# Output projection of a decoder layer on one NeuronCore: whole fp32 products, another order of token tiles, and earlier loads for the first two experts

## What is computed

```python
z = x @ w_in + b_in                       # q, k, v, conv pair, two gates
attn, conv = ...                          # dilated attention; depthwise conv
branch_c = silu(layer_norm(conv)) @ w_conv_out + b_conv_out
branch_a = attn @ w_attn_out
y = (g_a * branch_a + g_c * branch_c) @ w_o
h = layer_norm(DN_ALPHA * x + y)
# router: top 1 of 4 groups, then top 2 of its 8 experts, from fp32 logits
out = layer_norm(DN_ALPHA * h + moe(h))   # 32 SwiGLU experts, 1024 -> 512 -> 1024
```

## Time and profile before

| | us |
|---|---|
| median of 3 runs | 1113.03 (1111.85 to 1113.34) |
| profiled execution | 1111.08 |
| its span | 1109.3 |
| PE busy | 1021.5 (92%) |
| DVE busy | 624.5 (56%) |
| ACT busy | 286.8 (26%) |
| POOL busy | 217.2 (20%) |
| DMA queues, share of 16 engines | 69.3% |

### The profile page before, as it was taken

One profiled execution on the slowest core, in us unless ns is written; L12 is line 12 of the kernel. 1 busy time (PEld: TensorE's weight loads), 2 busy tenths in 40 slices (PEclk: granted clock), 3 DMA queues, 4 the chain that ended last, 5 costly groups with the idle time before them and its releaser, 6 DMA issues. The chain is left out here.

```text
span 1109.3 us, 30843 instructions
## 1 busy us (share of the span) xinstructions
PE 1021.5 (92%) x12960; PEld 792.5 (71%) x12960; DVE 624.5 (56%) x1386; ACT 286.8 (26%) x600; POOL 217.2 (20%) x193
## 2 busy tenths in 40 slices
PE   9999999999999899995999999999899998989880
PEld 8999998899997678874566665656565655656650
DVE  2699999810126728477367655445445453535435
ACT  3322321232225662011122222122121212212123
POOL 2453440232210014002111112111111212110100
PEclk9999999999998999996899999999999999999995
DMA  8467834136423521326999999999999999999624
GB/s 293 166 252 269 313 116 162 67 138 219 151 86 139 204 82 64 127 81 245 390 372 409 402 418 403 403 403 380 395 358 401 380 357 378 345 376 348 259 74 164
DMA packets 45696, 293.55 MB, mean 265 GB/s; under 512 B 11519, under 2 KB 15231, under 8 KB 26173
## 3 DMA queue, kind: packets, MB, share of 16 engines
q1 hardware_dynamic: 22285, 163.96, 38.3%
q10 hardware_dynamic: 12624, 102.63, 22.8%
q0 software_dynamic: 10720, 25.98, 7.9%
HBM read 286.83 MB, written 41.12 MB: 296 GB/s over the span
## 5 line engine op out<-in xcount | busy, mean ns | idle before, releaser
L978 PE MATMUL ps<-region_b,scratch 128*32 128x256 f32 x2976 | 174.7, 389 | 24.3 <-DMA region_b<-in_gate_up_rows 24.3
L978 PE MATMUL ps<-region_a,scratch 128*32 128x256 f32 x3168 | 180.3, 381 | 10.5 <-DMA region_a<-in_gate_up_rows 10.5
L995 PE MATMUL ps<-z_conv_gates,x_columns 128*32 128x256 f32 x3072 | 172.1, 379 | 0.0
L1718 DVE STREAM_TRANSPOSE scratch<-x_columns 32x256 f32<-32x256 f32 x384 | 165.8, 432 | 9.7 <-DMA x_columns<-h_rows,token_rows 3.6
L978 PEld LDWEIGHTS ps<-region_b,scratch 128*32 128x32 f32 x2976 | 107.5, 112 | 85.5 <-issue 26.3
L978 PEld LDWEIGHTS ps<-region_a,scratch 128*32 128x32 f32 x3168 | 113.8, 111 | 71.0 <-issue 15.8
L995 PEld LDWEIGHTS ps<-z_conv_gates,x_columns 128*32 128x32 f32 x3072 | 110.4, 110 | 55.3
L1375 DVE SCALAR_TENSOR_TENSOR z_conv_gates<-scratch,column_vectors,z_conv_gates 128x512 f32<-128x512 f32 x240 | 143.0, 673 | 0.0
L1724 DVE SCALAR_TENSOR_TENSOR x_columns<-ps,column_vectors,x_columns 128x128 f32<-128x128 f32 x96 | 33.7, 351 | 166.8 <-ACT x_columns L1272 165.0
L1272 ACT ACTIVATE x_columns<-ps 128x128 f32<-128x128 f32 x96 | 26.6, 277 | 377.6 <-PE ps L978 377.6
L579 PE MATMUL ps<-z_split,region_b_split 128*128 128x272 f32 x384 | 111.2, 290 | 0.0
(11 more groups left out here) (266 smaller groups left out, 1337.9 us busy)
## 6 DMA issues: line engine op xcount, KB each, us to landing
region_b<-in_gate_up_rows SPq DMA_DIRECT2D x21, 2048.0 KB
region_a<-in_gate_up_rows ACTq DMA_DIRECT2D x21, 2048.0 KB, 42.2
z_conv_gates<-in_down_rows SPq DMA_DIRECT2D x32, 1024.0 KB
z_conv_gates<-in_down_rows ACTq DMA_DIRECT2D x32, 1024.0 KB
region_a<-in_gate_up_rows SPq DMA_DIRECT2D x12, 2048.0 KB
region_b<-in_w_in_pairs SPq DMA_DIRECT2D x20, 1024.0 KB, 5.0
region_b<-in_gate_up_rows ACTq DMA_DIRECT2D x10, 2048.0 KB
region_b<-in_cache_tiles POOLq DMA_DIRECT2D x16, 768.0 KB, 4.9
```

Of the source, the lines that this page charges most:

```text
L978: last = pe.matmul(ps[j * R:(j + 1) * R, r, 0:2 * QF], ecols[s][:, r, 4 * c + k, :], w[:, k, j, :], start=c + k == 0, stop=c + k == 4)
L995: last = pe.matmul(ps[j * R:(j + 1) * R, RB + r, 0:QD], hcols[:, r, k * R:(k + 1) * R], w[:, k, j, :], start=k == 0, stop=k == KF - 1)
L1718: last = ve.transpose(ecols[s][q * R:(q + 1) * R, r, :, :].rearrange("p k c -> p (k c)"), xg[s][r * R:(r + 1) * R, q * QD:(q + 1) * QD])
```

## The change

- w_o is made in one fp32 product for each k (no high and low parts, no ACT casts and DVE subtractions). The sum of the two branches goes to `gc[m]`.
- The small tile is second: the tiles are now 128 (tile 0), 32 (tile 1), 128, 128, 128 rows. Its product is made in four column quarters of 256, one for each group of 32 PSUM partitions (`small_out`).
- Tiles 0 and 2 are made together, k by k, after all eight `br_used`. The norm of the last tile is no longer cut in two parts.
- Both gate-and-up halves of expert 1 are issued beside the second one of expert 0, after `merged` 6, and the down halves of experts 0 and 1 after `merged` 8. Gate and up and down of expert 2 still wait for `gathered[0]`.

The core of the diff:

```diff
-TILES = [(t * P, min(P, N - t * P)) for t in range((N + P - 1) // P)]
+SMALL = 1
+TILES = [(r * P, P) for r in range(SEQ // P)]
+TILES.insert(SMALL, (SEQ, NS))
...
                 if t == 1:

-                    sp_e.wait_ge(x_split, XQ + 6)
+                    sp_e.wait_ge(merged, 6)
                     load_gates(0, 0, 1)
-            sp_e.wait_ge(y_ps, NTT + 1)
-            for s in range(2):
-                sp_e.wait_ge(krow_stored[s], 16 * 3)
-            load_gates(1, 1, 0)
+                    load_gates(1, 1, 0)
+                    sp_e.wait_ge(merged, KD)
+                    for s in range(2):
+                        sp_e.wait_ge(krow_stored[s], 16 * 3)
+                    load_down(0, 0)
+                    load_down(1, 1)
+            sp_e.wait_ge(y_ps, NTT)

             sp_e.wait_ge(gathered[0], 16)
-            load_down(0, 0)
             load_gates(2, 2, 0)
-            load_down(1, 1)
             load_down(2, 2)
...
                     for k in ks:
-                        pe.matmul(out, ga_hi[k][:, c0:c0 + n], wo_hi[:, k, cols], start=k == 0, stop=False)
-                        pe.matmul(out, ga_hi[k][:, c0:c0 + n], wo_lo[:, k, cols], start=False, stop=False)
-                        last = pe.matmul(out, ga_lo[k][:, c0:c0 + n], wo_hi[:, k, cols], start=False, stop=k == KD - 1)
+                        last = pe.matmul(out, gc[k][:, c0:c0 + n], wo[:, k, cols], start=k == 0, stop=k == KD - 1)
+            def small_out():
+                c0, n = TILES[SMALL]
+                for k in range(KD):
+                    for j in range(GROUPS):
+                        last = pe.matmul(ps[j * R:(j + 1) * R, 6, 0:QD], gc[k][:, c0:c0 + n], wo[:, k, j * QD:(j + 1) * QD],
+                                         start=k == 0, stop=k == KD - 1)
+                return last
...
-            pe.wait_ge(br_used, KD - 1)
+            pe.wait_ge(br_used, KD)
+            pe.wait_ge(wo_loaded, 16)
             for k in range(KD - 2):
...
+                pe.wait_ge(merged, k + 1)
+                for t in (0, 2):
                     rows_out(t, [k])
+            pe.wait_ge(merged, KD)
+            rows_out(0, range(KD - 2, KD)).then_inc(y_ps, 1)
+            small_out().then_inc(y_ps, 1)
+            rows_out(2, range(KD - 2, KD)).then_inc(y_ps, 1)
+
+            turn_tile(0)
             pe.wait_ge(y_used, 1)
+            rows_out(3, range(KD), [0])
             logit_tile(0)
             turn_tile(1)
+            rows_out(3, range(KD), [1]).then_inc(y_ps, 1)
             logit_tile(1)
             turn_tile(2)
+            pe.wait_ge(y_used, 3)
+            rows_out(4, range(KD), [0])
             logit_tile(2)
             turn_tile(3)
+            rows_out(4, range(4), [1])
             logit_tile(3)
+            rows_out(4, range(4, KD), [1]).then_inc(y_ps, 1)
...
             norm_tile(0)
             norm_tile(1)
             norm_tile(2)
             route_tile(0)
+            norm_tile(3)
             route_tile(1)
-            norm_tile(3)
             route_tile(2)
+            route_tile(3)
             norm_tile(4)
             rank_tiles(0, NTT - 1, 1)
             route_tile(4)
...
-                po.tensor_tensor(ga[m], ga[m], gc[m], ALU.add).then_inc(merged, 1)
+                po.tensor_tensor(gc[m], ga[m], gc[m], ALU.add).then_inc(merged, 1)
```

More of the change, by code:

```diff
@@ L285, in build @@
         spare_row = route(NE)
-        COUNT_BANK = [3] * (NTT - 1) + [7]
-        LAST_ORDER = [NTT - 1, *range(NTT - 1)]
+        COUNT_BANK = [0] * (NTT - 1) + [6]
+        OUT_BANK = {0: 0, 2: 2, 3: 0, 4: 2}
+        LAST_ORDER = [SMALL, *(t for t in range(NTT) if t != SMALL)]
         unused_rows = z2[:, 0:D]
@@ L875, in logit_tile @@
                 for k in range(KD):
-                    last = pe.matmul(ps[0:n, 6 + t % 2, 0:36], hcol[:, k, 0:n], wrv[:, k, :], start=k == 0, stop=k == KD - 1)
+                    last = pe.matmul(ps[0:n, 7 - t % 2, 0:36], hcol[:, k, 0:n], wrv[:, k, :], start=k == 0, stop=k == KD - 1)
                 last.then_inc(lg_ps, 1)
@@ L883, in counts @@
                 for u in range(t):
-                    pe.matmul(out, onesb, mb[:, u, :], start=u == 0, stop=False)
+                    m = TILES[u][1]
+                    pe.matmul(out, onesb[0:m, :], mb[0:m, u, :], start=u == 0, stop=False)
                 return pe.matmul(out, beforeb[0:n, :], mb[0:n, t, :], start=t == 0, stop=True)
@@ L889, in listed @@
                 for k in range(2):
-                    last = pe.matmul(ps[0:BLK, 2, 0:NE], ohr_f[0:n, k * NTT + t, :], ohn[0:n, k, t, :],
+                    last = pe.matmul(ps[0:BLK, 1, 0:NE], ohr_f[0:n, k * NTT + t, :], ohn[0:n, k, t, :],
                                      start=t == 0 and k == 0, stop=t == NTT - 1 and k == 1)
@@ L951, in _ @@
             for t, (c0, n) in enumerate(TILES):
-                last = pe.matmul(ps[:, 3, NTT * NE:(NTT + 1) * NE], onesb[0:n, :], mb[0:n, t, :], start=t == 0, stop=t == NTT - 1)
+                last = pe.matmul(ps[:, 0, NTT * NE:(NTT + 1) * NE], onesb[0:n, :], mb[0:n, t, :], start=t == 0, stop=t == NTT - 1)
             last.then_inc(cnt_ps, 1)
@@ L1236, in _ @@
             columns_out(0)
+            root(2)
             columns_out(1)
-            for t in range(2, NTT):
-                root(t)
-                columns_out(t)
-            ac.wait_ge(y_ps, NTT + 1)
-            for s in range(2):
-                ac.wait_ge(krow_stored[s], 16 * 3)
-            def load_gates(e, s):
-                ac.dma_start(gu_place[s][1], gu_d[bass.ds(2 * e + 1, 1)].rearrange("o p x -> p (o x)")).then_inc(gu_loaded[s][1], 16)
-            def load_down(e, s):
-                ac.dma_start(dn_place[s][:, 2048:4096], dn_d[bass.ds(e, 1), 1].rearrange("o p x -> p (o x)")).then_inc(dn_loaded[s], 16)
-            load_gates(1, 1)
+            root(3)
+            columns_out(2)
+            columns_out(3)
+            root(4)
+            columns_out(4)
+            ac.wait_ge(y_ps, NTT)
             ac.wait_ge(rmax, 1)
```

113 lines of the change are left out of this document (36 added, 77 removed).

## The result

The changed kernel takes **1145.0 us** (median of 4 runs, 1137.7 to 1146.3), the one before, on the same chip, 1112.7 us: ratio 1.0273, 95% interval 1.0234 to 1.0312. By the ratio it is 30 us slower. The prediction, 1114.8 in a range of 1109.5 to 1119.5, missed. Executions far outside the rest (one of e1 with 1352.5 us, one of the kernel before with 3684.6 us) are left out of all comparisons.

What follows compares the result with a forecast made beforehand. PE was taken to eat a stock of weights, then go at the pace of HBM, with the DMA queues as the bound. A chain 8.2 us later less 6.4 us of stock put 1.8 on 1113.03: 1114.8 us, range 1109.5 to 1119.5.

Steps and rivals of the forecast that it cites:

- the base of the sum: Whole kernel before the change: median 1113.03 us, to which the forecast added its net.
- 8.2 - 6.4 us: Routing chain 8.2 us late, less 6.4 us taken for a stock of weights larger by 4.0 us.
- the first part: What bounds the kernel: PE takes 15.54 us per expert from 545 us, later 17.78 at the pace of HBM.
- the last rival: Early loads don't come early, or their traffic slows PE's instruction fetch: 8.2 us lost whole, 1121.2; chance 0.03.
- w_o stage: PE's w_o products: start 437.15, sum 67.0 us, end 504.1, no new stall inside.
- Chain and clock: After w_o, at half clock: turn 2.0, logits 3.6, row lists at 523.8, 8.2 us late.
- With the lead-in unchanged: Row lists to expert 3's load: stays 29.4 us, so that load is asked for at 553.2 instead of 545.0.
- Early loads: 10 MiB from about 428 us, done by 455; 4 MiB leave the later stream, stock larger by 4.0 us, worth 6.4.
- The hole in the traffic: DMA queues before expert 3's load: idle from about 547 to 553.2, some 6 us.
- First wait for weights at expert 12 to 14: Expert loop: sign of a right forecast, PE's first wait for weights at expert 12 to 14 instead of 10.
- The net, 1.8 us: Whole kernel: 8.2 us of later chain less 6.4 us of stock, 1.8 us later.
- the forecast's two nearest cases, 1114.8 and 1117.2: Whole kernel: forecast itself, 1114.8, chance 0.42; slower rival, stock worth only its 4.0 us, 1117.2, chance 0.33.

Runs made afterwards that it cites:

- e1: The change with 99 semaphore increments on PE in two gaps of the routing chain, loop body back at place 138; 1124.6 us.
- e13: The change with 49 products of 16 columns and one increment behind keep_running, loop body at place 138; 1117.3 us, ratio 1.0052 to the kernel before.
- e2: The kernel before with 157 semaphore increments on PE in three gaps, loop body at place 39 as in the change; 1145.7 us.
- e7: e8 with both early moves taken back: expert 1's gates after the last `y_ps`, downs of 0 and 1 after the gather; 1121.1 us.
- e8: The change with the loops of PE and SP over experts 3 to 26 written out; 1113.5 us.
- e6: The kernel before with the loops of PE and SP over experts 3 to 26 written out; 1111.2 us.
- e9: e8 with PE kept busy by products in the gaps of the routing chain; 1110.0 us.
- e5: The change with keep_running's 20 products of 512 columns replaced by 69 of 148, and one increment, body at 138; 1118.2 us.
- e10: e9 with expert 2's gates also asked for at the last `y_ps`; 1110.0 us.

## Why the prediction was wrong

**The step that failed** is the base of the sum, the 1113.03 us of the kernel before, to which only 8.2 - 6.4 us were added. It takes for granted that PE's loop keeps the pace stated in the first part: "PE goes through one expert in 15.54 us, without a pause", and later the pace of the loads. The text of the loop is the same, so a change of its pace got no term, and the prediction gives no reason for that. The runs showed 9.8 us more than 15.54 each in every pass from 627 us on, by fetches of the loop body, which left 30 us when the former waits for weights are taken off. 25 of the 30 go with the loop's place (e13 against the change), and the kernel before gets the same waits when its loop is moved to the same place (e2). I had named the mechanism in the last rival, "or their traffic slows PE's instruction fetch", but as an effect of the early loads, with a chance of 0.03 for both its cases and a price, 8.2 us, that was only the loss of what the early loads bring. It has nothing to do with the early loads: they are over by 455, and e2 has none of them. The sign was there to be read: the page of before has a q8 line, its list for 700 to 800 us has none, and a loop whose body does not reload is one that could.

Point by point:

- **w_o stage: right.** Start 436.0 (437.15), last group ends 504.45 (504.1), and no stall inside. The 1.7 us wait for the eighth `br_used` came as 1.58. The two changes of tile form show no gap: the small tile's products run from 460.24 to 463.90 us, the groups beside them end at 460.31 and start at 463.83. No run from before shows the 0.858 us that the sum takes for a whole fp32 product of 512 columns; the 0.432 us for a round of the small tile is a quarter of the 1.73 us between the first two starts of the earlier trace rows. The changed kernel showed 0.859 us for a product of 512 columns (eight from 486.15 to the logits at 493.02, clock 1.00), 0.865 over the first 28, and 0.449 us for each of the small tile's eight rounds (460.24 to 463.83).
- **Chain and clock: right.** Turn 1.97, logits 3.63, lists at 523.85. The gather was over, and the first load behind it asked for, at 529.06, 8.1 us later than before.
- **"With the lead-in unchanged": wrong by 3.8 us**, the other way. It took 549.50 - 523.85 = 25.65 us, not 29.4. Before, L962 began at 517.38 and its last 16 products at 526.99, and its records hold 3.7 us of waits for issue, the last of them this:

```profile
526.99 0.60 PE L962 MATMUL ps<-w_attn,value_rows 128*32 128x32 f32 x16 [2.56 <-issue]
```

  In the change that group has one of 0.24. A wait for issue, by my estimate for a late block as in the loop, had been in rows 11, and I counted it as work. Expert 3 came 4.5 us late, not 8.2. The prediction overstated this term.
- **Early loads: right in size as far as measured.** The stretch from 437 to 450 us moved 423 GB/s, from 450 to 455 213. Both moves together are worth 7.6 us, give or take 3.4 (e7 against e8), where 6.4 was taken from 4.0 to 7.7 for the down halves alone. The hole in the traffic was smaller than forecast: a share of 0.86 from 545 to 553, where some 6 of these 8 us were to be empty.
- **First wait for weights at expert 12 to 14:** the changed kernel has none. Written out, in e8, the first are at 726.82 and 744.51, experts 12 and 13.
- **The net, 1.8 us:** 2.0 measured with the loop written out, give or take 2.4. With the loop kept and its place restored (e13) it is 5.8 (3.6 to 7.9), of which the padding explains some 1.8. What is left between the two pairs, 2 us, is within their intervals. So the forecast's two nearest cases, 1114.8 and 1117.2, are both open. That 2.0 agrees with 1.8 is in part luck: the sum had expert 3's load 3.7 us too late, a hole in the traffic that was hardly there, and nothing for the early gates.

One pair of runs bears on what the working held to matter most. e6 asks for expert 3 at 536.37, 8.6 us before its rolled sibling, of which its trace had 2.2 before the routing chain (its last w_o product is at 499.09, not 501.29). Its first load behind the gather is 2.4 us earlier (518.56 against 520.93), and it ends 1.2 us earlier, too little to tell from no change. That suggests that the time of expert 3's load counts for little beside the time at which the stream of loads begins and the bytes that it has to bring; a run that moves only that load was not made.

## What to carry over

A change that adds or removes instructions anywhere ahead of a loop on an engine moves the loop's body in the instruction stream. Where the body is large (here 1764 instructions on PE), compare the instruction queue's packets and the "issue" waits before and after, ahead of any reasoning on the work itself. If a loop turns out to be fetched anew in each pass, write it out or shift it by cheap instructions (a smaller body was not tried here), and time an unchanged kernel with the same shift before you blame an edit. Judge an edit by the difference between two kernels whose loops are in the same state: here that turned a loss of 30 us into one of 2 to 6. And a wait that a change adds is worth only what it exceeds the waits that it replaces: nearly 70 us of late instructions cost 30, since some 42 had been lost before, mostly to late weights.

## What was unexpected of the hardware

- A loop body of 1764 PE instructions, 6.9 packets of 16 KB, goes through 8 passes with no fetch after the first when it begins at place 126 or 138 of 256, and fetches about 9 packets in each later pass at 10, 39 or 115. The jump back spans 6.9 packets, and at place 138 (e13) no packet came from 630 to 1000 us. Written out, in e8, blocks followed each other unnoticed for a while: 11 packets from 630 to 700 us, no wait.
- In straight code PE waits for issue for 2.5 to 3.6 us in some traces shortly after the first loads behind the gather are asked for (2.56 before, 3.55 in e1 and e9, 2.53 in e5, 3.47 in e10; one q8 packet moved in each of these waits), 0.2 to 1.4 in others (the change, e8, e7), and nothing some 100 us later in e8 with the queues as full.
- A semaphore increment on PE, as an instruction of its own, costs 0.14 us (8.36 us for 60), a matmul of 16 bf16 columns 0.03 us (1.37 us for 49), so matmuls are the cheaper padding.
